# Mixer heads of a two-layer transformer block: conditioning products, key reciprocal and bounds' softmax put at other places in the instruction order

## The reference

```python
p = u @ w_mix_in[l]                        # the projection: 29 tiles of 128 columns
p_conv, p_hg, p_rw = jnp.split(p, (CONV_PROJ, CONV_PROJ + HG_PROJ), axis=-1)
y = jnp.concatenate([short_conv_mixer(p_conv, ...), hgrn2_mixer(p_hg, lb_all[l], ...),
                     rwkv7_mixer(p_rw, ...)], axis=-1)
h = h + y @ w_mix_out[l]

# hgrn2_mixer: the lower bounds are a softmax over the two layers (zero for layer 0)
lb_sm  = jax.nn.softmax(hgrn_lb_logits, axis=0)
lb_all = jnp.maximum(jnp.cumsum(lb_sm, axis=0) - lb_sm[0], 0.0)
log_f  = jax.nn.log_sigmoid(f_logit) + jnp.log1p(lb * jnp.exp(jnp.minimum(-f_logit, 80.0)))

# rwkv7_mixer: the keys are scaled to length one, head by head
kk = heads(k * k_k)
kk = kk / jnp.maximum(jnp.sqrt(jnp.sum(kk * kk, axis=-1, keepdims=True)), 1e-12)

# second block: one matrix product per layer makes the conditioning vector
mod = jax.nn.silu(c) @ w_mod[l] + b_mod[l]     # 1024 x 6144, independent of the first block
```

## Time and profile before

| | |
|---|---|
| median of three executions | 3812.21 us |
| the profiled execution | 3820.85 us |
| span of its one core | 3819.1 us |
| mean granted TensorE clock | 0.949 |
| TensorE matmul busy | 3473.7 us (91%) |
| VectorE busy | 2765.2 us (72%) |
| ScalarE busy | 1228.8 us (32%) |
| GpSimd busy | 434.2 us (11%) |

### The profile page before, as it was taken

One profiled execution on the slowest core, in us unless ns is written; L12 is line 12 of the kernel. 1 busy time (PEld: TensorE's weight loads), 2 busy tenths in 40 slices (PEclk: granted clock), 3 DMA queues, 4 the chain that ended last, 5 costly groups with the idle time before them and its releaser, 6 DMA issues.

```text
span 3819.1 us, 51712 instructions
## 1 busy us (share of the span) xinstructions
PE 3473.7 (91%) x20728; PEld 2840.2 (74%) x20728; DVE 2765.2 (72%) x3178; ACT 1228.8 (32%) x1628; POOL 434.2 (11%) x453
## 2 busy tenths in 40 slices
PE   8997979999996979998789999999669789999995
PEld 8995778999994778996555767676557666767674
DVE  8887577888887577876757777777463777777774
ACT  1013111101014111011323656565320345656562
POOL 0000100101001100101001212122110011212120
PEclk9998889999998889999899999999889899999998
DMA  6444333454544333451024999999632169999993
GB/s 242 178 167 168 117 134 121 174 195 177 180 159 159 125 122 133 177 188 66 1 108 178 367 369 360 358 360 369 249 126 98 45 240 340 337 348 333 338 337 129
DMA packets 118800, 799.25 MB, mean 209 GB/s; under 512 B 33808, under 2 KB 34832, under 8 KB 48400
## 3 DMA queue, kind: packets, MB, share of 16 engines
q1 hardware_dynamic: 76752, 709.97, 50.5%
q0 software_dynamic: 40752, 84.77, 6.2%
q10 hardware_dynamic: 1040, 1.05, 0.1%
HBM read 808.77 MB, written 71.83 MB: 231 GB/s over the span
## 4 chain that ended last, share of the span: by engine, by line
PE 78%; DVE 16%; ACT 3%; issue 2%; DMA 1%; POOL 0%; DVEq 0%; POOLq 0%; ACTq 0%; SPq 0%
PE ps L374 44%; PE ps L1930 30%; PE ps L1940 3%; DVE ring_r L136 3%; DVE arena L406 3%; DVE arena L414 1%; DVE ring_r L135 1%; ACT arena L422 1%; DMA arena<-yd_dram 1%; DVE ring L406 1%; DVE arena_r L406 1%; PE ps L1978 1%; DVE arena_r L414 1%; DVE arena L465 1%; ACT arena L426 1%
## 5 line engine op out<-in xcount | busy, mean ns | idle before, releaser
L374 PE MATMUL ps<-arena_r,ring_r 128*128 128x256 f32 (+1 forms) x10224 | 1314.4, 290 | 81.4 <-DVE ring_r L136 26.7
L374 PEld LDWEIGHTS ps<-arena_r,ring_r 128*128 128x128 f32 x10224 | 1273.4, 191 | 119.6 <-DVE arena L406 28.0
L1930 PE MATMUL ps<-ring_r,arena_r 128*128 128x512 f32 x1864 | 550.4, 397 | 0.9 <-DVE arena_r L1946 0.9
L136 DVE TENSOR_TENSOR ring_r<-ring,ring_r 128x4096 fp32r<-128x4096 f32 (+2 forms) x121 | 510.4, 4218 | 10.5 <-ACT ring_r L133 6.4
L422 ACT ACTIVATE arena<-arena 128x256 f32<-128x256 f32 (+3 forms) x295 | 143.7, 487 | 1101.1 <-DVE arena L406 803.5
L1930 PE MATMUL ps<-ring,arena 128*128 128x512 f32 x1032 | 464.0, 593 | 1.0 <-DVE arena L1982 1.0
L1927 DVE TENSOR_TENSOR ring_r<-ring,arena_hi 128x2048 fp32r<-128x2048 f32 x154 | 353.1, 2293 | 98.1 <-ACT arena_hi L1926 89.7
L1930 PE MATMUL ps<-arena_hi,arena_r 128*128 128x512 f32 x1232 | 407.6, 398 | 0.0
L1930 PEld LDWEIGHTS ps<-ring_r,arena_r 128*128 128x128 f32 x1864 | 347.9, 189 | 74.1 <-DVE arena_r L1946 1.4
L1930 PEld LDWEIGHTS ps<-ring,arena 128*128 128x128 f32 x1032 | 195.8, 190 | 197.0 <-issue 185.0
L374 PE MATMUL ps<-arena 128*128 128x128 f32 (+5 forms) x1728 | 261.7, 334 | 85.7 <-DMA arena<-yd_dram 42.3
(11 more groups left out here) (184 smaller groups left out, 3349.3 us busy)
## 6 DMA issues: line engine op xcount, KB each, us to landing
ring<-wexp_dram SPq DMA_DIRECT2D x387, 1024.0 KB, 8.3
ring<-stream_dram SPq DMA_DIRECT2D x143, 2048.0 KB, 7.7
arena<-yd_dram POOLq DMA_DIRECT2D x12, 2048.0 KB, 10.5
xd_dram<-arena POOLq DMA_DIRECT2D x6, 512.0 KB, 10.0
consts_sb<-consts_dram SPq DMA_DIRECT2D x1, 2241.5 KB, 16.3
arena<-xd_dram,small POOLq DMA_INDIRECT x129, 10.5
yd_dram<-arena,small POOLq DMA_INDIRECT x129, 8.3
arena<-mem_dram POOLq DMA_DIRECT2D x2, 1024.0 KB, 5.2
```

What stands on the lines that cost most here:

```text
L136: toks.append(self.dve(lambda e, h=h, r=r, w=w: e.tensor_tensor(w, r, h.bitcast(F32), ALU.subtract), t))
L374: return PE(lambda e: e.matmul(ps, lhsT=lhsT, rhs=rhs, start=start, stop=stop, skip_group_check=True), *after, inc=inc)
L1930: return P(lambda e: e.matmul(out_, lhsT=x, rhs=y, start=st_, stop=sp_, skip_group_check=True), *after, inc=inc)
```

## The change

Four things, all by place in the program:

1. `FILL.step(1)` at the head becomes `FILL.step(4)`, and 0.75 in the loop of 18 becomes 0.625. So the two clears, the first eight products and the first row copy stand ahead of "roots".
2. The one reciprocal of 128x768 becomes three of 128x256, each a piece of its own ("inverse"), with plan numbers 25, 26 and 27.
3. "sums" goes from plan number 25 to 23 and hgrn's "logs" from 23 to 24.
4. In layer 1, the three small VectorE instructions and the Exp that begin the bounds' softmax become a piece "limits" with number 10. The rest of the softmax stays where it was.

```diff
@@ mixer
-            plan = [..., (8, rb, "low"), (13, rb, "decay"), (15, rb, "rate"),
-                    (17, rb, "gates"), (19, rb, "scan"), (20, rb, "scanned"), (21, rb, "squares"), (23, ha, "logs"),
-                    (25, rb, "sums")]
+            plan = [..., (8, rb, "low"), (10, ha, "limits"), (13, rb, "decay"), (15, rb, "rate"),
+                    (17, rb, "gates"), (19, rb, "scan"), (20, rb, "scanned"), (21, rb, "squares"), (23, rb, "sums"),
+                    (24, ha, "logs"), (25, rb, "inverse"), (26, rb, "inverse"), (27, rb, "inverse")]
...
             FILL.start(modulation(l, f))
-            FILL.step(1)
+            FILL.step(4)
             upto(rb, "roots")
...
             for i in range(18):
                 upto(rb, "inverse")
                 upto(ha, "level")
-                FILL.step(0.75)
+                FILL.step(0.625)
@@ hgrn
+            if l == 1:
+                s = small
+                tl = tt(DVE, s[:, 0:3], par("lbl", 0, 0, 3), par("lbl", 1, 0, 3), ALU.max)
+                tl = tt(DVE, s[:, 3:6], par("lbl", 0, 0, 3), s[:, 0:3], ALU.subtract)
+                tl = tt(DVE, s[:, 6:9], par("lbl", 1, 0, 3), s[:, 0:3], ALU.subtract)
+                tlim = act(s[:, 9:15], s[:, 3:9], ACT.Exp, tl)
+            yield "limits"
             act(T1.v(), Fl, ACT.Abs, (DVE, DVE.n))
...
-                te = act(s[:, 9:15], s[:, 3:9], ACT.Exp, tl)
-                tl = tt(DVE, s[:, 15:18], s[:, 9:12], s[:, 12:15], ALU.add, te)
+                tl = tt(DVE, s[:, 15:18], s[:, 9:12], s[:, 12:15], ALU.add, tlim)
@@ rwkv
             yield "sums"
-            t = DVE(lambda e: e.reciprocal(EMe.v(), EMe.v()), te)
+            for j in range(3):
+                ej = EMe.v(256 * j, 256)
+                t = DVE(lambda e, ej=ej: e.reciprocal(ej, ej), te)
+                yield "inverse"
```

More of the change, by code:

```diff
@@ L688, in mixer @@
             rb = rwkv(l, P, Y, Yr, wk, W2G2[:, 0:384], W2G2[:, 384:768], wa, spare, ytok, f)
-            plan = [(4, cv, "padded"), (5, cv, "block"), (6, cv, "block"), (8, rb, "low"), (13, rb, "decay"), (15, rb, "rate"),
-                    (17, rb, "gates"), (19, rb, "scan"), (20, rb, "scanned"), (21, rb, "squares"), (23, ha, "logs"),
-                    (25, rb, "sums")]
+            plan = [(4, cv, "padded"), (5, cv, "block"), (6, cv, "block"), (8, rb, "low"), (10, ha, "limits"), (13, rb, "decay"), (15, rb, "rate"),
+                    (17, rb, "gates"), (19, rb, "scan"), (20, rb, "scanned"), (21, rb, "squares"), (23, rb, "sums"),
+                    (24, ha, "logs"), (25, rb, "inverse"), (26, rb, "inverse"), (27, rb, "inverse")]
             def also(p):
@@ L792, in hgrn @@
             if l == 1:
-                s = small
-                tl = tt(DVE, s[:, 0:3], par("lbl", 0, 0, 3), par("lbl", 1, 0, 3), ALU.max)
-                tl = tt(DVE, s[:, 3:6], par("lbl", 0, 0, 3), s[:, 0:3], ALU.subtract)
-                tl = tt(DVE, s[:, 6:9], par("lbl", 1, 0, 3), s[:, 0:3], ALU.subtract)
-                te = act(s[:, 9:15], s[:, 3:9], ACT.Exp, tl)
-                tl = tt(DVE, s[:, 15:18], s[:, 9:12], s[:, 12:15], ALU.add, te)
+                tl = tt(DVE, s[:, 15:18], s[:, 9:12], s[:, 12:15], ALU.add, tlim)
                 tl = DVE(lambda e: e.reciprocal(s[:, 15:18], s[:, 15:18]))
```

## The result

| | before | after |
|---|---|---|
| median of seven executions each | 3814.02 us (3809.03 to 3817.96) | 3824.26 us (3821.58 to 3831.97) |
| ratio, 95% interval | | 1.0031 [1.0021, 1.0041] |
| the profiled execution, its span | 3820.85, 3819.1 us | 3822.28, 3820.5 us |
| mean granted TensorE clock | 0.949 | 0.952 |
| TensorE matmul busy | 3473.7 us | 3465.9 us |

A forecast was written before the change was run, and what follows sets the result against it. The prediction took TensorE as the bound, but VectorE's or ScalarE's chain in the head. Layer 0's +4.65 and layer 1's +2.4 made +7.0 us on 3812.2, so 3819.2 us; own range 3816.5 to 3822, outer range 3811 to 3826.

The forecast's parts named there:

- "sums" in layer 0: Layer 0's projection: TensorE reaches the moved matmuls before VectorE's "squares" product is ready, loss 6.1 us.
- The clock behind that wait: Layer 0's projection: TensorE's lower clock after the wait costs 1.45 us, bounds nothing and twice that.
- Layer 0's head: Last copy to keys' product: shorter VectorE chain given back by ScalarE's, -0.4 us, bounds +0.25 and -1.15.
- Loop and tail: Loop of 18 and tail: less filler on TensorE, 2.5 us less per layer, bounds 2.0 and 3.5.
- "limits": Layer 1's projection: three small VectorE instructions and a second table load cost 1.84 us, bounds 0.6 and 3.0.
- that rival: ScalarE pays the skill's drain on the sigmoids' table load in layer 1, +1.3 us, 3820.5 us; chance 0.03.
- "sums" in layer 1: Layer 1's projection: TensorE reaches the matmuls before VectorE's product ends, loss 1.6 us, bound 3.0.
- Layer 1's head: From the last copy through the product after Ln: net +1.45 us, or +0.05 with fast products.
- the high ends: Both layers: clock and heads cost most, loops give 2.0 us each; +11.5 us, 3823.7 us; chance 0.19.
- "Faster": ScalarE and TensorE don't wait at the moved instructions, only removals count; -10.2 us, 3802 us; chance 0.06.

The follow-up runs named there:

- e3: Kernel before with only "sums" moved to 23 and "logs" to 24; 3828.45 us, ratio 1.0036 to before.
- e8: The change with "sums" at 24, "logs" at 25 and "inverse" at 26, 27, 28; 3820.76 us, ratio 1.0023 to before.
- e2: The change with "sums" back at 25, "logs" at 23 and "inverse" at 26, 27, 28; 3816.67 us, ratio 1.0013 to before.
- e7: e6 with "logs" at 23, "sums" plus first reciprocal at 25, "inverse" at 26 and 27, "limits" joined to "logs"; 3800.98 us, ratio 0.9974 to before.
- e9: Kernel before with only the head's FILL.step(4), the loop staying at 0.75; 3812.73 us, ratio 0.9998 to before.
- e11: e7 with the six identity copies made by GpSimd instead of ScalarE; 3803.15 us, ratio 0.9973 to before.
- e10: Kernel before with only the loop's 0.625, the head staying at FILL.step(1); 3807.78 us, ratio 0.9991 to before.
- e4: Kernel before with only the filler's edit, FILL.step(4) at the head and 0.625 in the loop; 3810.75 us, ratio 0.9997 to before.
- e5: Kernel before with only "limits" at 10 in layer 1; 3814.87 us, ratio 1.0006 to before.
- e6: The change with the row copy's filler step moved from the head to behind "mixed"; 3812.82 us, ratio 1.0001 to before.
- e1: The changed kernel run again unedited, which gave the second trace of the change; 3822.12 us, ratio 1.0023 to before.

## Why the prediction was right, and which terms were off

**"sums" in layer 0: right.** Forecast 6.1 us of wait, measured 6.08, in e3 alone 6.07, in e8 3.25, in e2 none.

**The clock behind that wait: the mis-sized term.** "I take these 1.45 us again" failed. E moved by 9.3 us, and the first matmuls had started 0.16 earlier; less the wait of 6.1 that leaves 3.4 (2.9 in the second trace). Both places where it went can be read: 1.6 in the sums matmuls, which take 3.31 us from their start to the next tile (294.19 to 297.50) for 1.75 before, and 1.79 in the five tiles behind (16.14 for 120 / 192 of 22.96; 1.3 in the second trace). The upper bound, 2.9, was twice the row of layer 1, and the first trace lies above it as well: I had priced the tiles and left out that the sums matmuls themselves run at 1.2 GHz.

That row of layer 1 was also less firm than it looked. The same 192 matmuls behind the same wait of 3.4 us took 24.4 us in before, e7, e9 and e11, 25.36 in e10 and 22.88 in e4, which is no loss at all. Behind the wait of 4.62 us they took 24.20 in e2 and 25.61 in e5, and the 168 of the change 21.46 in its first trace and in the second:

```profile
1116.78 22.78 PE L374 MATMUL ps<-arena_r,ring_r 128*128 128x256 f32 x168 [4.62 <-DVE arena L406]
```

At the full clock 168 take 20.09 us (168 / 192 of 22.96). So what the clock costs behind a wait was a range of 0 to 2.7 us for tiles alone, and no run shows that it grows with the wait.

**Layer 0's head: right to the keys' product, and then incomplete.** Forecast -0.4, measured -0.43 and +0.16; the eight products ahead of the row copy took 2.7 and 3.3 us, inside the bounds that I had set. e6 shows that the row copy was the reason. But scan to loop, which no term priced, took 4.2 and 3.7 us more. On the timeline of after, ScalarE:

```profile
330.80 0.59 ACT L426 COPY mrow<-ps 128x512 f32<-128x512 f32 x1
...
340.30 0.59 ACT L426 COPY mrow<-ps 128x512 f32<-128x512 f32 x1 [2.99 <-PE ps L374]
```

The second row's copy (330.80) stands behind the identity copies, TensorE's folds wait 5.72 us for it and run slowly, the third row's copy (333.39) waits 2.00 us for them, and the fourth's (340.30) another 2.99, with hgrn's activations behind each. e4 (+2.2), e10 (+0.4) and e11 (-0.5) agree: it takes the longer filler in the head and the identity copies in front of it. I had stopped following ScalarE's queue at the keys' product. From E to the loop the head costs 3.8 us more than before in both traces of the change and 0.3 more in e6: what the first row copy held up, the late square root with the Exp and identity copies behind it, makes up nearly all of the head's loss.

**Loop and tail: the forecast's -2.5 was right in sign and wrong in its mechanism.** "2.0 us less on TensorE, which is the chain there" rested on the earlier trace rows. The records do go from 568 to 552. The windows over layer 0's loop, of before and of after:

```profile
355.21:420.47 65.26, 62.58 (x568) 53.81 (x568) 44.47 (x69) 16.49 (x29) 20.34 (x16) 0.95 0.27 98
...
420.47:448.22 27.75, 24.88 (x146) 21.60 (x146) 10.73 (x16) 3.84 (x6) 3.30 (x2) 0.69 0.21 77
```

```profile
368.33:433.02 64.69, 60.45 (x552) 52.19 (x552) 44.45 (x69) 15.88 (x28) 20.37 (x16) 0.97 0.26 94
433.02:457.03 24.01, 21.18 (x139) 19.02 (x140) 10.74 (x17) 3.84 (x6) 3.30 (x2) 0.79 0.04 16
```

TensorE is busy 2.1 us less, the loop is 0.6 shorter, and in the second trace of the change it is 0.7 longer than before (65.93). The chain of waits of after says why:

```profile
369.69 8.20 PE ps L374 x64
377.89 0.58 DVE arena L955
...
382.25 2.05 PE ps L374 x16
...
384.43 12.37 PE ps L374 x116
396.80 0.58 DVE arena L955
...
401.15 2.05 PE ps L374 x16
...
403.33 28.44 PE ps L374 x268
```

The one piece of 62.63 us has become five, with two stretches of VectorE among them, from 377.89 to 382.25 and from 396.80 to 401.15, 8.7 us. With less filler TensorE runs out of work and the loop's own dependency through VectorE ends last. Not all of the 8.7 us is lost: TensorE itself waits 1.3 us there, in two waits, and that is most of the 1.5 by which the gain falls short of 2.1. The second trace is longer for another reason, the clock at the loop's start: its first 64 matmuls took 9.47 us for 8.20. A chain that is one engine's for 62 us said what bounded the loop, not by how much: here taking 2.1 us off was enough to put VectorE on it.

What did become shorter is the stretch behind the loop, on nearly the same instructions: 27.75 us at a granted clock of 0.69 to 24.01 at 0.79, and in the second trace of the change:

```profile
433.91:453.03 19.12, 16.30 (x139) 14.14 (x140) 10.72 (x17) 3.84 (x6) 3.30 (x2) 1.00 0.05 19
```

In layer 0 the kernels with 0.625 in the loop had 19.12 at 1.00 (e1, e6, e7, e10), 22.4 at 0.85 (e11) or 24.0 at 0.79 (the first trace of the change, e2, e4, e8); in layer 1 from 21.97 at 0.92 (e7) to 27.98 at 0.70 (e1). Those with 0.75 (before, e3, e5, e9) had 26.4 to 27.8 in layer 0 and 28.7 to 30.7 in layer 1. So in all thirteen traces the loop's number parts the two groups, in both layers, without overlap. Length times clock is 19 to 20.6 us in the traces given here with both, so this is clock, which the forecast did not speak of. Why it takes these values within a group stays open. The tail gave 1.4 and 1.1 us in layer 0, 0.0 and 0.5 in layer 1; 0.5 was forecast.

**"limits": right up to the restart.** +1.84 forecast, +1.87 in all kernels that have it at 10. The clock behind the longer wait had no term: nothing more in the first trace, 1.3 us in the second, 1.2 in e5. The Trainium skill ("ScalarE: Activation LUTs", section "What ACT_TABLE_LOAD costs") adds a drain of 1.38 us to every load; the load at 1109.20 ends at 1110.48 and the sigmoids start at 1110.49, so the trace shows none, and that rival falls.

**"sums" in layer 1: right.** 1.6 forecast, 1.70 and 1.69 measured. Restart to E grows by 1.8 and, in the second trace, 3.1; the 1.3 between them lie in the 168 matmuls ahead of "sums", behind the wait of "limits".

**Layer 1's head: right, a little low.** +1.45 forecast, +1.73 in both traces. ScalarE waited 4.80 us at the row copy (the slow products that I had taken, 3.7 us for the 3.3 priced), and e6, without that copy there, is 5.4 us shorter.

**The sum.** Up to the end of layer 0's tail the traces have +7.4 and +3.8 us, forecast +4.65; over layer 1 -2.5 and +2.5, forecast +2.4; together +4.9 and +6.3 for 7.0, timed +10.2 and +9.2. What was missing on the cost side is the clock behind the wait (+1.9 and +1.5 over the term) and scan to loop (+4); what was missing on the other is the clock behind the loop, -3.7 us in layer 0 and -8.0 in layer 1 (second trace -8.6 and -2.7), in place of the 2.0 that I took for each loop. These misses have opposite signs and are each about as large as the forecast itself, so that the sum came within 3.2 us is in part luck. The measured 3824.3 lies above the forecast's own range of 3816.5 to 3822 and inside the outer one. Since the timed runs lie above the traces' difference, either the changed kernel's usual execution gives back less there than these two traces do, or the one trace of before is long in the first block as well as in the second; it stays open which. What is shown by timing is the parts: the row copy's place 9.7 us (e1 against e6), the three waits together with the shifted reciprocals 11.8 (e6 against e7). Of my rivals the high ends, 3823.7 us, came nearest. "Faster" was ruled out by the wait. That e7 has 3801.0 us, where this rival said 3802, is luck: in e7's trace the loop and the stretch behind it give 7.9 and 8.7 us, where the rival had 2.5 per layer, and E to loop in layer 0 gives nothing, where it had 3.2.

## What to carry to other kernels

An early place for an instruction pays only if its operand is ready there: before moving a small matmul or copy up in an in-order queue, read on the timeline when its producer ends, and count everything queued behind it plus the time at the low clock after the idle, as a range read from more than one trace. Follow each queue that the moved piece enters, ScalarE's above all, down to the next stage and not only to the instruction one has in view. And where a chain is all one engine's, work taken from it is worth only what the second chain lags: look for the next releaser before pricing it.

## What the runs showed of the hardware that I had not expected

- The cost in clock of an idle TensorE between dense tiles did not follow the length of the wait. Tiles alone lost 0 (e4), 1.45 (before, e7, e9, e11) and 2.4 us (e10) behind 3.4 us, 1.2 behind 3.25 (e8), 1.2 to 2.7 behind 4.62, 1.3 to 1.9 behind 6.1, 0.2 (the change) and 1.6 (e3) behind 1.7. Three matmuls of "sums" right behind the wait lost another 1.5 to 1.6 in each of five traces of layer 0.
- The same 139 matmuls in a sparse stretch took 19.12 us at a granted clock of 1.00 and (layer 1) 27.98 at 0.70; the 284 of the tail 40.65 at 0.81 and 49.21 at 0.68. In these traces the filler's place changed the time more through this than through its own length.
- Untouched code, the second block, took 3.5 to 5.8 us less in the two traces of the change than in that of before, several times the 1.4 us between the two profiled executions.
